# Hybrid decoder layer on one Trainium2 core: first loads in halves with idle ones products ahead, less filler before the first DeltaNet sums, key's sum a chunk later, last sum as two products

## The reference

```
h = rms_norm(x, g0);  p = h @ w_in + b_in            # split into the branches' columns
y_b: q, k, v = silu(conv4(.)); q, k l2-normalised per head (4 heads of 128);
     chunked gated delta rule; rms_norm over the head; times silu(z)
y_a: gMLP spatial gating;  y_c: stick-breaking attention (8 heads)
mixed = sum_i(sigmoid(gate_i) * (y_i @ w_branch_i)) @ w_out
x = x + rms_norm(mixed, g1)
f = square(relu(rms_norm(x, g2) @ w_ff1)) @ w_ff2
x = x + rms_norm(f, g3)
```

## Time and profile before

| | |
|---|---|
| median of three runs | 1978.13 us |
| the profiled execution, its own time | 1978.7 us |
| span of its instructions | 1976.8 us |
| PE (TensorE) busy | 1934.8 us, 98% of the span |
| DVE busy | 941.1 us, 48% |
| ACT busy | 758.9 us, 38% |
| GpSimd busy | 82.8 us, 4% |
| chain of waits that ended last | PE 93%, DVE 3%, DMA 2%, ACT 1%, issue 1% |

### The profile page before, as it was taken

The page is one execution under the profiler, slowest core; times in us unless marked ns, Lnnn a source line. Parts: engine busy times, 40 slices in busy tenths (PEclk is TensorE's granted clock), DMA queues, the critical chain, the costliest instruction groups (busy, mean ns, idle before and its releaser), DMA issues.

```text
span 1976.8 us, 25186 instructions
## 1 busy us (share of the span) xinstructions
PE 1934.8 (98%) x9812; PEld 1572.5 (80%) x9812; DVE 941.1 (48%) x1266; ACT 758.9 (38%) x1163; POOL 82.8 (4%) x63
## 2 busy tenths in 40 slices
PE   8999999998999999999999999999999999999996
PEld 6887777776878888788787888888888888888885
DVE  6715566674435454523446554774333223223446
ACT  6335555554353433533334344543232113202331
POOL 0000000000202122120000000000000000000000
PEclk9999999999999999999999999999999999999998
DMA  5223122213122221222524444432211111111144
GB/s 186 103 100 115 49 97 100 92 60 128 65 96 86 96 86 54 78 83 102 186 100 163 149 142 145 150 133 96 98 52 53 53 42 46 50 53 42 59 144 149
DMA packets 62048, 191.75 MB, mean 97 GB/s; under 512 B 6720, under 2 KB 6784, under 8 KB 61952
## 3 DMA queue, kind: packets, MB, share of 16 engines
q1 hardware_dynamic: 59648, 186.23, 27.1%
q10 hardware_dynamic: 2304, 4.20, 0.6%
HBM read 146.33 MB, written 44.07 MB: 96 GB/s over the span
## 4 chain that ended last, share of the span: by engine, by line
PE 93%; DVE 3%; DMA 2%; ACT 1%; issue 1%; SPq 0%; DVEq 0%; ACTq 0%
PE gemm L339 18%; PE gemm L341 17%; PE gemm L340 17%; PE gemm L582 5%; PE gemm L584 5%; PE gemm L583 5%; PE dn L1319 2%; PE dn L1317 2%; PE z L1216 2%; PE gemm L1404 2%; PE dn L1238 2%; PE gemm L1406 2%; PE gemm L1405 2%; PE dn L1280 1%; PE dn L1315 1%; PE attn_out L1250 1%
## 5 line engine op out<-in xcount | busy, mean ns | idle before, releaser
L339 PE MATMUL gemm<-act_hi,w_hi 128*128 128x512 f32 x1216 | 501.8, 413 | 0.8 <-issue 0.5
L341 PE MATMUL gemm<-act_hi,w_lo 128*128 128x512 f32 x1216 | 476.0, 391 | 0.0
L340 PE MATMUL gemm<-act_lo,w_hi 128*128 128x512 f32 x1216 | 475.1, 391 | 0.0
L331 DVE TENSOR_TENSOR w_lo<-w_raw,w_hi 128x1024 fp32r<-128x1024 f32 x174 | 213.3, 1226 | 189.3 <-ACT w_hi L326 185.8
L326 ACT ACTIVATE w_hi<-w_raw 128x1024 fp32r<-128x1024 f32 x174 | 183.1, 1052 | 285.8 <-PE gemm L341 153.2
L341 PEld LDWEIGHTS gemm<-act_hi,w_lo 128*128 128x128 f32 x1216 | 228.8, 188 | 49.5
L339 PEld LDWEIGHTS gemm<-act_hi,w_hi 128*128 128x128 f32 x1216 | 229.8, 189 | 47.0 <-issue 7.2
L340 PEld LDWEIGHTS gemm<-act_lo,w_hi 128*128 128x128 f32 x1216 | 230.0, 189 | 43.2 <-issue 3.8
L385 ACT ACTIVATE stage<-gemm,cols 128x512 f32<-128x512 f32 x104 | 71.6, 689 | 213.9 <-PE gemm L341 209.4
L1088 ACT ACTIVATE f_t<-f_t 128x512 f32<-128x512 f32 x64 | 40.4, 632 | 218.0 <-DVE f_t L1916 218.0
L1586 DVE TENSOR_TENSOR_SCAN a_P<-a_keep,a_P,a_floor 128x512 f32<-128x512 f32 (+3 forms) x96 | 94.0, 1007 | 37.6 <-ACT a_keep L883 37.3
(11 more groups left out here) (272 smaller groups left out, 2880.2 us busy)
## 6 DMA issues: line engine op xcount, KB each, us to landing
w_raw<-w_stream SPq DMA_DIRECT2D x174, 512.0 KB, 3.4
projections<-stage SPq DMA_DIRECT2D x60, 512.0 KB, 2.9
gate<-projections SPq DMA_DIRECT2D x48, 256.0 KB, 2.8
d_in<-projections SPq DMA_DIRECT2D x12, 512.0 KB, 7.1
x_sb<-xT SPq DMA_DIRECT2D x8, 512.0 KB, 9.2
x_fin<-xT SPq DMA_DIRECT2D x8, 512.0 KB, 4.3
residual<-mixed ACTq DMA_DIRECT2D x16, 256.0 KB, 2.0
act_hi<-residual SPq DMA_DIRECT2D x8, 512.0 KB, 4.9
```

What stands on the lines that cost most here:

```text
L331: nc.vector.tensor_tensor(lo[s][:], raw[s][:].rearrange("p (k c) -> p k c", k=KT), hi[s][:].bitcast(f32), ALU.subtract).then_inc(lo_ready[ ...
L339: nc.tensor.matmul(g_bank[hf][:], w_hi[s][:, k, :], a_hi[:, k, t], start=(k == 0), stop=False)
L340: nc.tensor.matmul(g_bank[hf][:], w_hi[s][:, k, :], a_lo[:, k, t], start=False, stop=False)
L341: last = nc.tensor.matmul(g_bank[hf][:], w_lo[s][:, k, :], a_hi[:, k, t], start=False, stop=(k == KT - 1))
```

## The change

Four edits.

1. *Start.* PE makes 20 products of the ones matrix with itself (128 columns, result unused, in the bank `c_bank`) as soon as the matrix is set, and four more between the first two products of tile 0 of the first block. The two first weight blocks are loaded and split in halves of four tiles, in the order weights 0 (first half), x tile 0, weights 1 (first half), x tile 1 (each 256 KB), weights 0 (second half), x tiles 2 and 3, weights 1 (second half), x tiles 4 and 5, and so on. The second halves are split in front of tiles 2 and 3. The counters `bank_read` are raised before these loads are issued. Four semaphores of a later phase are used a second time, so their later waits count from a higher value.
2. *Prologue of the DeltaNet.* `DN_PRO` becomes `[12, 3, 8]`: the first three slots end at steps 11, 14 and 22, and all later ones move by four steps, falling to one or none in the last head. `root_of(0, 0)` on ACT moves ahead of the second slot.
3. *Scan.* The key's sum moves from behind chunk 3 to behind chunk 4.
4. *End.* DVE no longer adds the sixteenth square. PE multiplies the sum of fifteen by ones, and then, into the same bank, the sixteenth square.

```diff
-        def split_hi(act, n, s, first=False, free=False):
+        def split_hi(act, n, s, free=False):
...
+        def first_piece(t, part):
+            return t[:, HALF * part:HALF * part + HALF].rearrange("p (k c) -> p k c", c=P)
+
+        def first_hi(act, s, part):
+            act.wait_ge((first_raw, raw_loaded)[part][s], 16)
+            nc.scalar.activation(fw_hi[s][:, 4 * part:4 * part + 4, :], first_piece(f_raw[s], part), ACT.Copy).then_inc(
+                hi_ready[s] if part else first_up, 1)
+
+        def first_lo(dve, s, part):
+            dve.wait_ge(*((hi_ready[s], 1) if part else (first_up, s + 1)))
+            k = slice(4 * part, 4 * part + 4)
+            nc.vector.tensor_tensor(fw_lo[s][:, k, :], first_piece(f_raw[s], part), fw_hi[s][:, k, :].bitcast(f32),
+                                    ALU.subtract).then_inc(lo_ready[s] if part else first_low, 1)
...
-        DN_PRO = [13, 6, 8]
+        DN_PRO = [12, 3, 8]
...
+        WARM = 20
...
+            for one in bank_read:
+                sp.sem_inc(one, 1)
+
+            def load_first(s, part):
+                c = slice(HALF * part, HALF * part + HALF)
+                sp.dma_start(f_raw[s][:, c], w_stream[0, s][:, c]).then_inc((first_raw, raw_loaded)[part][s], 16)
+
+            load_first(0, 0)
+            sp.dma_start(x_sb[:, 0, 0:HALF], xT[0, :, 0:HALF]).then_inc(x_first, 16)
+            load_first(1, 0)
+            sp.dma_start(x_sb[:, 1, 0:HALF], xT[1, :, 0:HALF]).then_inc(x_in[0], 16)
-            for r in range(8):
+            for r in range(1, 8):
...
-                if r in (0, 1):
-                    load_weights(sp, 0, r, first=True)
+                if r < 3:
+                    load_first(r - 1, 1)
...
-                    if hf == 0 and k in (0, 1):
-                        split_hi(act, 0, k, first=True)
-                    act.wait_ge(x_in[4 * hf + k // 2], 16)
+                    if hf == 0 and k in (0, 2, 3):
+                        first_hi(act, max(0, k - 2), 1 if k else 0)
+                    if (hf, k) == (0, 0):
+                        act.wait_ge(x_first, 16)
+                    else:
+                        act.wait_ge(x_in[4 * hf + k // 2], 16)
...
+                    if (hf, k) == (0, 0):
+                        first_hi(act, 1, 0)
...
             beside()
+            root_of(0, 0)
             beside()
-            root_of(0, 0)
             root_of(0, 1)
...
             pe.wait_ge(ones_set, 1)
+            for n in range(WARM):
+                nc.tensor.matmul(c_bank[:, 0:P], ones[:], ones[:], start=True, stop=True)
...
                         nc.tensor.matmul(o, fw_hi[s][:, k, :], pre_hi[:, k, t], start=(k == 0), stop=False)
+                        if first and s == 0:
+                            for n in range(4):
+                                nc.tensor.matmul(c_bank[:, 0:P], ones[:], ones[:], start=True, stop=True)
...
-                    if n in (2, 3) and i < 3:
-                        pe.wait_ge(dn_sq, 2 * i + 2 + n - 1)
+                    if n in (2, 4) and i < 3:
+                        j = n // 2 - 1
+                        pe.wait_ge(dn_sq, 2 * i + 2 + j + 1)
                         for g in range(2):
-                            squares_sum(g, d_r[n - 2], dn_use(i, NDS + n - 2))
+                            squares_sum(g, d_r[j], dn_use(i, NDS + j))
...
-            total_of(pe, 1, sum_sq, (e_added, 1 + 16), e_total)
+            pe.wait_ge(e_added, 1 + 15)
+            nc.tensor.matmul(d_bank[1][:], ones[:], sum_sq[:, half_of(1)], start=True, stop=False)
+            pe.wait_ge(e_sq, 16)
+            nc.tensor.matmul(d_bank[1][:], ones[:], n_sq[1][:], start=False, stop=True).then_inc(e_total, 1)
...
-                    if hf == 0 and k in (0, 1):
-                        split_lo(dve, 0, k, first=True)
+                    if hf == 0 and k in (0, 2, 3):
+                        first_lo(dve, max(0, k - 2), 1 if k else 0)
...
+                    if (hf, k) == (0, 0):
+                        first_lo(dve, 1, 0)
...
-                    dve.wait_ge(e_sq, 8 * hf + b + 1)
-                    dve.wait_ge(e_added, 1 + 8 * hf + b)
-                    nc.vector.tensor_tensor(sum_sq[:, t], sum_sq[:, t], n_sq[s][:], ALU.add).then_inc(e_added, 1)
+                    if 8 * hf + b < 15:
+                        dve.wait_ge(e_sq, 8 * hf + b + 1)
+                        dve.wait_ge(e_added, 1 + 8 * hf + b)
+                        nc.vector.tensor_tensor(sum_sq[:, t], sum_sq[:, t], n_sq[s][:], ALU.add).then_inc(e_added, 1)
```

More of the change, by code:

```diff
@@ L283, in hybrid_decoder_layer @@
         gate_sig = [sem(f"gate_sig{s}") for s in range(2)]
+        first_raw, x_first, first_up, first_low = g_load, gw_load, g_masked, g_root
         m_added, mh_ready, ml_ready = sem("m_added"), sem("mh_ready"), sem("ml_ready")
@@ L312, in leave_phase, with load_weights @@
             pe.drain().then_inc(phase, 1)
-        def load_weights(sp, n, s, first=False, back=0):
-            if not first:
-                sp.wait_ge(lo_ready[s], n)
-            sp.dma_start((f_raw if first else w_raw)[s][:], w_stream[n - back, s]).then_inc(raw_loaded[s], 16)
-        def split_hi(act, n, s, first=False, free=False):
+        def load_weights(sp, n, s, back=0):
+            sp.wait_ge(lo_ready[s], n)
+            sp.dma_start(w_raw[s][:], w_stream[n - back, s]).then_inc(raw_loaded[s], 16)
@@ L322, in split_hi @@
+        def split_hi(act, n, s, free=False):
             act.wait_ge(raw_loaded[s], 16 * n + 16)
-            if not (first or free):
+            if not free:
                 act.wait_ge(blk_done[s], n)
-            raw, hi = (f_raw, fw_hi) if first else (w_raw, w_hi)
-            nc.scalar.activation(hi[s][:], raw[s][:].rearrange("p (k c) -> p k c", k=KT), ACT.Copy).then_inc(hi_ready[s], 1)
-        def split_lo(dve, n, s, first=False):
+            nc.scalar.activation(w_hi[s][:], w_raw[s][:].rearrange("p (k c) -> p k c", k=KT), ACT.Copy).then_inc(hi_ready[s], 1)
@@ L329, in split_lo @@
+        def split_lo(dve, n, s):
             dve.wait_ge(hi_ready[s], n + 1)
-            raw, hi, lo = (f_raw, fw_hi, fw_lo) if first else (w_raw, w_hi, w_lo)
-            nc.vector.tensor_tensor(lo[s][:], raw[s][:].rearrange("p (k c) -> p k c", k=KT),
-                                    hi[s][:].bitcast(f32), ALU.subtract).then_inc(lo_ready[s], 1)
+            nc.vector.tensor_tensor(w_lo[s][:], w_raw[s][:].rearrange("p (k c) -> p k c", k=KT),
+                                    w_hi[s][:].bitcast(f32), ALU.subtract).then_inc(lo_ready[s], 1)
@@ L605, in _ @@
             sp.dma_start(cols[:, 0:V_LNG], cols_in[:, 0:V_LNG]).then_inc(g_loaded, 16)
-            for r in range(8):
+            for one in bank_read:
[8 more added lines that the diff above has]
+            for r in range(1, 8):
                 hf, q = divmod(r, 4)
                 t = slice(HALF * hf, HALF * hf + HALF)
-                if r in (0, 1):
-                    load_weights(sp, 0, r, first=True)
+                if r < 3:
+                    load_first(r - 1, 1)
                 sp.dma_start(x_sb[:, 2 * q:2 * q + 2, t], xT[2 * q:2 * q + 2, :, t].rearrange("k p s -> p k s")).then_inc(x_in[r], 16)
-            for one in (*bank_read, *stored, dn_yst, *dn_taken, *y_stored, at_read, av_done, ml_ready, f_lr):
+            for one in (*stored, dn_yst, *dn_taken, *y_stored, at_read, av_done, ml_ready, f_lr):
                 sp.sem_inc(one, 1)
@@ L1152, in _ @@
                         if first:
-                            pe.wait_ge(hi_ready[s], 1)
+                            pe.wait_ge(first_up, s + 1)
+                        if (hf, k) == (0, 4):
+                            pe.wait_ge(lo_ready[s], 1)
                         if s == 0:
@@ L1369, in _ @@
             pe_beside(pe, b8)
-            pe.wait_ge(g_masked, 1)
+            pe.wait_ge(g_masked, 3)
             for b in range(4):
@@ L1768, in _ @@
             b8 = Beside(PAIR_SG, SG_SLOTS, (ACT.Identity,) * 4)
-            dve.wait_ge(g_load[0], 16)
+            dve.wait_ge(g_load[0], 32)
             nc.vector.tensor_tensor(g_sum[:], g_v[:, 0, :], g_v[:, 1, :], ALU.add).then_inc(g_added, 1)
-            dve.wait_ge(g_load[1], 16)
+            dve.wait_ge(g_load[1], 32)
             for b in range(2, 4):
@@ L1807, in normal @@
                 nc.vector.tensor_scalar(n[:], n[:], cols[:, V_LNB + b:V_LNB + b + 1], None, ALU.add).then_inc(g_normed, 1)
-            dve.wait_ge(g_root, 1)
+            dve.wait_ge(g_root, 3)
             normal(0)
@@ L2029, in _ @@
             end_phase(pool, 3)
-            pool.wait_ge(gw_load, 16)
+            pool.wait_ge(gw_load, 32)
             nc.gpsimd.tensor_tensor(g_w[:], g_w[:], up_incl[:, None, :].broadcast_to([P, 8, P]), ALU.mult).then_inc(g_masked, 1)
```

2 lines of the change are left out of this document (1 added, 1 removed).

## The result

The changed kernel takes 1963.7 us (median of four runs, 1963.0 to 1964.5) against 1978.4 us for the kernel before, run beside it (1977.7 to 1979.5, four runs): ratio 0.9927, 95% interval 0.9914 to 0.9939, so 0.73% less; the medians differ by 14.7 us. In a later series five runs gave 1962.4 us (1961.7 to 1964.9), ratio 0.9925 (0.9912 to 0.9939). The forecast was 1961.0 us, with a range of 1958.0 to 1966.5. The profiled execution took 1964.2 us with a span of 1962.4, against 1976.8 before. PE is now busy for 1936.0 us, 99% of the span.

A forecast was written before the change was run, and what follows sets the result against it. PE, busy for 98% of the span, was taken as the bound, so only its waits and low-clock time could be regained: 2.5 + 6.6 + 5.6 + 2.4 = 17.1 us, giving a median of 1961.0 us, range 1958 to 1966.5.

The forecast's parts named there:

- Start: Kernel start: first ones product at 20.0 instead of 22.55 us, a gain of 2.5 us.
- Prologue: DeltaNet prologue: `gram` at 477.5 instead of 486.89 with four steps still to do, a gain of 6.6 us.
- Scan: Heads 1 and 3: waits before the key's sum and head 1's lower clock go, a gain of 5.6 us.
- End: Last sum: PE stands about 0.6 us and the final logarithm starts earlier, a gain of 2.4 us.
- PE follows the producers from tile 3 on: Start: tile 3's lower part at 13.1 us, then PE is slower at 1.37 per tile, reaching the ones product at 20.0.
- Rival 3: Start: the warming products do nothing for PE, as producers or clock still rule; 1963.5 us, chance 0.12.
- The step count: Prologue: three steps after the query's sums, eight after the key's until 477.5, four (2.75 us) left for later.
- the order of ACT's logarithms: Prologue: ACT makes two logarithms of 0.69 us before the weight split, so the first bank is free at 470.3.
- the pause: Prologue: PE stands 1.9 us before the key's sum, without lowering the clock.
- rival 1: Prologue: the 1.9 us pause lowers the clock; 1963.1 us, chance 0.15.
- Rival 2: Scan: head 1's gap only moves, the key's sum still finding its bank taken; 1965.5 us, chance 0.08.
- Rival 4: Scan: the key's root comes too late for DVE in chunk 5, stopping PE in heads 1 to 3; some 1990 us, chance 0.02.

The follow-up runs named there:

- a_whole: Changed kernel with its first weights and x tiles loaded whole in the old order, splits still in halves: 1964.11 us, ratio 0.9932 to the kernel before.
- b_nostart: Kernel before with the prologue, scan and end edits but not the start's: 1965.69 us, ratio 0.9937 to the kernel before.
- b_nostart_spread: b_nostart with the sixteen small 8-column products spread over four steps of the next block: 1969.04 us, ratio 0.9945 to the kernel before.
- s_prologue: Kernel before with the prologue's edit alone (new DN_PRO and query's root moved): 1968.12 us, ratio 0.9946.
- s_start: Kernel before with the start's edit alone (idle products, halved loads and splits, early counters): 1980.22 us, ratio 1.0011.

## Why the prediction was right, and where it was off

It was right in direction and in range, 2.7 us too fast in its middle (1961.0 against 1963.7; 1.4 against the later series). The mechanism held in three of the four edits; the term that was mis-sized is the start.

**Start, 2.5 us forecast, 1.0 measured.** The reading that PE follows the producers from tile 3 on held: from 14.82 to 21.54 it took 6.72 us, where 13.1 to 20.0 was forecast, 6.9. The mis-sized term is the time of tile 3's lower part, 13.1 in the forecast and 14.77 in the profile. It goes back to the landing times. I had put the halves at 4.1, 4.9 and 5.8 us; they came at 5.22, 6.05 and 8.12. x tile 1, forecast for 6.95, landed at 8.76 (6.1 us from issue), and tiles 2 and 3, forecast for 9.1, let ACT wait until 10.80. So the lower part of tile 1 ended at 10.88 and not at 8.9, while the 4.2 us from there to tile 3 were 3.9. The early stretch moved fewer bytes than before (4 to 5 us, the changed kernel and then before; the last column is GB/s):

```profile
4.00:5.00 1.00, 1.00 (x8) 1.00 (x8) 0.00 (x0) 0.00 (x0) 0.00 (x0) 1.00 0.61 113
```

```profile
4.00:5.00 1.00, 0.00 (x0) 0.00 (x0) 0.00 (x0) 0.05 (x1) 0.00 (x0) 1.00 0.90 260
```

I had charged no loss to the halves because the queue was full from 10 to 12 us. That rate does not hold in the first 5 us. It is the halves that lower it: the five profiles with them have 61 to 113 GB/s from 4 to 5 us, the eight with the old start 244 to 289, and a_whole, with the idle products and whole loads, 277:

```profile
4.00:5.00 1.00, 1.00 (x6) 1.00 (x6) 0.00 (x0) 0.00 (x0) 0.00 (x0) 1.00 0.95 277
```

The sentence of the Trainium skill that I had weighed (DMA: Bandwidth & Descriptors, section Measured: transfers of 1 MiB and more, for at least 75% of the peak; its table is for loads issued from GpSimd) would have given 1.5 instead of 2.5. The landings agree with its direction. The 1.0 us of the profile is not its doing, though: with whole loads (a_whole) the first ones product stands at the same place (21.62 against 21.54).

What holds tile 3 back in both is DVE's list. Before, one whole split was done while DVE had nothing else, and the other stood ahead of tile 1; after, two half splits stand ahead of tiles 2 and 3. The listing before and after:

```profile
9.59 1.23 DVE L331 TENSOR_TENSOR act_lo<-f_raw,act_hi 128x1024 fp32r<-128x1024 f32 x1 [0.53 <-ACT act_hi L326]
...
13.33 0.75 DVE L1468 SCALAR_TENSOR_TENSOR pre_lo<-x_sb,cols,pre_hi 128x512 fp32r<-128x512 f32 x1
```

```profile
10.13 0.75 DVE L1509 SCALAR_TENSOR_TENSOR pre_lo<-x_sb,cols,pre_hi 128x512 fp32r<-128x512 f32 x1 [0.65 <-ACT sq L850]
...
11.40 0.69 DVE L343 TENSOR_TENSOR act_lo<-f_raw,act_hi 128x512 fp32r<-128x512 f32 x1
...
13.41 0.68 DVE L343 TENSOR_TENSOR act_lo<-f_raw,act_hi 128x512 fp32r<-128x512 f32 x1
```

From tile 1's lower part to tile 3's it is 2.54 us before (10.79 to 13.33) and 3.89 after (10.13 to 14.02). The edit brought tile 1 0.7 us earlier and tile 3 0.7 us later; the first ones product gained only because PE had less left to catch up.

Also, 22.55 us was a late draw. In the eight profiles with the old start the first ones product stands between 21.2 and 22.9, mean 21.9, since PE's pace rises at another time in each: at 14.45 us before, at about 12.0 in b_nostart, with the same code. In the six with the new start it is 20.9 to 21.7, mean 21.5. The edit's own gain there is thus about 0.4 us. The Trainium skill (TensorE: Matmul & The Clock Gate, Part 1) says that the number of slow matmuls at a kernel's start varies from run to run; the traces agree, with a rise 6.25 us after the first product in one and about 3.7 in the other. Rival 3, that the idle products do nothing for PE, holds at the start. Its time, 1963.5, is also the nearest to the measured one, though it gave the start nothing at all, and the stretch outside the sum has its share in that.

**A stretch outside the sum, 1.6 us.** I took everything between the start and the prologue as unmoved, and by the runs the change does not move it. The clock's fall near 130 us was in the profile of before and I passed over it; its length varies by chance, and an execution of the changed kernel can lose 1.6 us there or not. The forecast allowed 1 us of this kind.

**Prologue, 6.6 forecast, 6.6 measured.** The step count, the order of ACT's logarithms and the pause (1.9 forecast, 1.61) held, and rival 1 fell, since the pair behind it ran at full pace. The margin was thin: the forecast had only a gap of 1.12 on the safe side, 2.0 us left the pace as it was in b_nostart, and behind 2.18 us it fell in b_nostart_spread. But the number is only that of this stretch: the edit is worth 10.3 us alone, as it also shortens head 1's gap.

**Scan, 5.6 forecast, 5.7 in the heads of the whole and 6.3 alone.** Rival 2 (the gap only moves) fell: no wait over 0.3 us came before the key's sum. The fit in the heads is in part luck, as other waits there changed as well (2.1 us of them gone, 2.8 new). I gave the shorter ACT chain of head 1 to this term, and s_prologue shows that it is the prologue's edit that brings it (0.76 us left with the sum unmoved). Once the prologue's edit is made, the scan's adds about 1 us in the profiles: from `gram` of head 0 to that of head 1 it is 114.23 us before, 112.59 with the prologue's edit alone and 111.46 in the changed kernel. In the ratios not even that can be told: prologue and end alone multiply to 0.9935 (0.9946 x 0.9989), and with the scan's edit beside them (b_nostart) it is 0.9937. Rival 4 (slower) didn't come: of the waits for `d_vn` one of 0.9 us is left. So two terms of the sum are not what each edit is worth: the prologue's edit is worth 10.3 us and the scan's, beside it, about 1.

**End, 2.4 forecast, 2.3 measured and 2.2 alone.** PE stands 0.58 us, 0.6 forecast; the logarithm follows after 1.16, with 1.06 forecast.

## What to carry to other kernels

Two edits that each take the cause of the same wait away don't add up, and an edit can lose alone and not lose beside others: price each with the others made, and run both ways. Filling PE with idle products, or splitting the first loads, brings nothing at the start while a chain of other engines sets the pace; ask first which tile's producer PE joins for good, and what the edit itself puts into that producer's list. A term of one us read from a single profiled execution should be checked against a second one, since stretches with changes of the clock differ from one execution to the next, by 1.6 us between two of the changed kernel.

## What the runs showed of the hardware

- The granted clock fell to 0.50 while PE was listed as busy without a break, for about 3.5 or 7 us in the same code (129 to 138 us), and for 7 to 10 us with the products of 8 columns spread out. Waiting is not the only thing that lowers it. Pauses of 1.1, 1.6 and 2.0 us (b_nostart, pair listed with 1.98) left the pace as it was; those of 2.2 (b_nostart_spread, pair listed with 2.58), 2.8 and 2.9 us did not. After the last of these the clock was back after 7 us in s_start, after that of 2.8 us in the kernel before after 3.5.
- First loads of 256 KB instead of 512 KB moved 61 to 113 GB/s from 4 to 5 us, against 277 with whole loads in the same kernel (a_whole).
- Kernels with and without edits in the first 10 us differed hundreds of us later: in the landing of one weight load (8.5 to 9.8 us with the start's edit, 7.4 to 8.5 without) and, with the new prologue list, in the crossing of a phase boundary (2.1 us with the idle products, 2.8 to 3.7 without). Both stay without an explanation.
